# Moving the split weights and one raw buffer by 32 bytes within a partition

## The chip, the cores and the metric

The kernel runs on one core of a Trainium2 chip. The metric is the device time of one execution in microseconds (us); the lower, the better. Two such numbers are compared by the median of their runs. TensorE is the matrix engine (PE in the profile, PEld its weight loads), VectorE (DVE), ScalarE (ACT) and GpSimd (POOL) are the others, and SyncE (SP) issues the DMAs.

## The reference, cut to what matters

Two blocks run one after the other on 256 tokens of width 1024, all in fp32. The first is a convolution mixer and a mixture of 32 experts, the second has two layers of three kinds of attention, a cross attention to a memory, and a gated feed-forward part. The change touches only the second block, where nearly all work is products of the tokens with large weights:

```python
for l in range(DEPTH_2):                       # 2 layers
    xn = rmsnorm_2(x, norm_mix[l])
    (qa, ka, va, ..., gates) = jnp.split(xn @ w_in[l], offsets, axis=-1)      # 1024 x 8004
    ...                                        # attention A, B, C
    y = (g[:, :, 0] * (o_a @ w_up_a[l]) + g[:, :, 1] * (o_b @ w_up_b[l])
         + g[:, :, 2] * (o_c @ w_up_c[l]))
    x = x + y @ w_out[l]
    x = x + memory_cross_attention(rmsnorm_2(x, norm_cross[l]), mem_n, ...)
    x = x + swiglu(rmsnorm_2(x, norm_ffn[l]), w_gu[l], w_down[l])             # 1024 x 5632, 2816 x 1024
return rmsnorm_2(x, final_norm)
```

## The kernel before

Tokens are kept transposed: the 128 partitions hold channels, the free dimension holds the 256 tokens. Each product of the second block is made from parts of the fp32 operands that TensorE takes in its float32r form: a weight chunk is split into a high part (`w_hi`) and the rest (`w_lo`), the tokens into `h_hi` and `h_lo` (both in the tensor `h_parts`) or, in the feed-forward part and for two of the three attention outputs, `act_hi` and `act_lo` (`act_parts`). Three matmuls then stand for one: high x high, low x high, high x low.

The weights come in 35 pieces per layer, each up to 2 MB, by SyncE's queue into three raw buffers in turn: two lie in `raw_a`, the third is `raw_b`. A piece is cut into chunks of 128 x 1024. For each chunk ScalarE copies the raw numbers to `w_hi` (L1616), VectorE, or GpSimd for 26 of the chunks, writes the difference to `w_lo` (`low_part`, L636), and TensorE reads both. `w_hi` and `w_lo` hold four chunks each (`PARTS`). `WORK_SPLIT` is an order written out by hand, the same for all engines, and semaphores (`w_hi_ready`, `w_lo_ready`, `chunk_used`) hold them together.

The lines that read split weights: L990, L991 and L993 (`split_chunk`), L1021 to L1083 (the first products behind a norm), L1416 to L1418 (values, with the tokens as the stationary operand and 512 weight columns moving), L1522 to L1526 (`up`), L1594 to L1597 and L1384 to L1386 (`down`). Two lines read raw buffers as plain fp32: L1546 and L1553 `raw_a`, L1568 `raw_b`.

In the first block the experts' weights stream through `ring` (six slots of 16 KB in a partition) and two spare places, the tensors `wp` and `hs`. L1259 and L1324 multiply them with gathered tokens. The gather (L1222) and the scatter (L1249) are float32r products of which both operands lie in `moe_parts`. `ring` is freed before the tensors of the second block are laid out, so these lie in the same bytes: slot 0 is `w_lo`, slot 1 `w_hi`, slot 2 `raw_b`, slot 3 about `h_parts`, slots 4 and 5 about `raw_a`. Tensors are laid out one behind the other in the order of the `sb(...)` calls. In bytes of a partition they begin at:

| tensor | begins at | rest of a division by 64 |
|---|---|---|
| `ring`, `w_lo` | 1152 | 0 |
| `w_hi` | 17536 | 0 |
| `raw_b` | 33920 | 0 |
| `h_hi` (in `h_parts`, 50304, plus 8 elements) | 50336 | 32 |
| `raw_a` | 66752 | 0 |
| `hs` | 107712 | 0 |
| `act_parts`, `moe_parts` and `big` (one place, at different times) | 145056 | 32 |
| `outs` | 194208 | 32 |
| `wp` | 206496 | 32 |

`H_SHIFT` is 8 elements, 32 bytes. `view(t, at, ...)` gives a part of a tensor from element `at` on, in the shape asked for.

Of the kernel before, what the change touches and what calls it, by code (L numbers as in the profile page):

```python
# [11 lines left out]
F32R = mybir.dt.float32r  # L12
# [6 lines left out]
P = 128  # L19
SEQ = 256  # L20
D = 1024
KD = D // P
# [26 lines left out]
PARTS = 4  # L49
# [4 lines left out]
H_SHIFT = 8  # L54
# [283 lines left out]
def build(nc, x, mem, cst, vec1, vec2, relpad, w_in, w_out, w1, w3, w2, w_in_2, w_up_a, w_up_b, w_up_c,  # L338
# [12 lines left out]
    with ExitStack() as ctx:  # L351
        def sb(name, shape, dt=F32):
            return ctx.enter_context(nc.sbuf_tensor(name, shape, dt))
# [4 lines left out]
        def view(t, at, *dims):  # L358

            n = int(np.prod(dims))  # L360
            ap = t[:, at:at + n]
            if len(dims) == 2:
                return ap.rearrange("p (a b) -> p a b", a=dims[0])
            if len(dims) == 3:
                return ap.rearrange("p (a b c) -> p a b c", a=dims[0], b=dims[1])
            return ap
# [4 lines left out]
        with ExitStack() as first_block:  # L371

            ring = first_block.enter_context(nc.sbuf_tensor("ring", [P, RING, PIECE], F32))
        w_lo = sb("w_lo", [P, PARTS, KD * P], F32R)
        w_hi = sb("w_hi", [P, PARTS, KD * P], F32R)
        raw_b = sb("raw_b", [P, PIECE])
        h_parts = sb("h_parts", [P, 2 * KD * SEQ + 2 * H_SHIFT], F32R)
        h_hi, h_lo = (view(h_parts, H_SHIFT + i * KD * SEQ, KD, SEQ) for i in range(2))
        raw_a = sb("raw_a", [P, RAW - 1, PIECE])
        xT = sb("xT", [P, KD, SEQ])  # L380
        hs = sb("hs", [P, 2 * KD * SEQ])
# [2156 lines left out]
```

How the kernel before makes its waits and increments, by code:

```python
        def enter(eng, name, l=0):  # L556
            d, n = seats[name]
            eng.wait_ge(duo_free[d], l * layer_tenancies[d] + n + 1)
# [1 line left out]
        def freed(eng, name, l=0):  # L561
            d, n = seats[name]
            eng.wait_ge(duo_free[d], l * layer_tenancies[d] + n + 2)
# [7 lines left out]
        def done_piece(eng, i):  # L572
            if i < 2:
                eng.wait_ge(half_done, i + 3)
            else:
                eng.wait_ge(piece_done, i - 1)
# [1 line left out]
        def arrived(eng, i):  # L578
            eng.wait_ge(ring_full[MIX_SLOTS[i]], MIX_SLOTS[:i + 1].count(MIX_SLOTS[i]) * 16)
# [9 lines left out]
        def rotate(eng, r, l):  # L589
            sines, turned_sines = rope_parts(r)
            eng.wait_ge(rope_tmp, l * 5 + r + 1)
            if r >= 2:
                eng.wait_ge(rope_ready, l * 5 + r - 1)
            for at in range(0, P, 32):
                eng.dma_start(turned_sines[at:at + 32], sines[at ^ 32:(at ^ 32) + 32]
                              ).then_inc(rot_odd if r % 2 else rot_even, 16)
# [1 line left out]
        def rotation_in(eng, r, l):  # L600
            if r % 2:
                eng.wait_ge(rot_odd, (l * 2 + r // 2 + 1) * 64)
            else:
                eng.wait_ge(rot_even, (l * 3 + r // 2 + 1) * 64)
# [4 lines left out]
        def raw_arrived(eng, i, l):  # L610
            so_far = sum(LOADS[j] for j in range(i % RAW, i + 1, RAW))
            a_layer = sum(LOADS[j] for j in range(i % RAW, N_LAYER, RAW))
            eng.wait_ge(raw_full[i % RAW], (l * a_layer + so_far) * 16)
```

## Time and profile before

| | us |
|---|---|
| median of 3 runs | 1640.3 |
| lowest and highest | 1639.52, 1641.46 |
| the profiled execution | 1638.12 |
| its span, first to last instruction | 1636.1 |
| TensorE busy | 1562.6 (96%) |
| VectorE busy | 893.3 (55%) |
| ScalarE busy | 651.5 (40%) |

A page of the profile has the busy times, the span in 40 slices, and the chain of work that ended last. Groups of instructions carry their line in the kernel, out<-in by tensor name, the shapes, the count, the time busy and the mean duration of one in ns. A matmul is pipelined: the next one begins before the last has ended, so the mean duration is not the time that one more costs. For that the timeline is read, which gives the start of each instruction; where equal instructions follow each other, one row merges them, with their count and the time from the first start to the last end.

### The profile page before, as it was taken

The numbers are of one execution on the slowest core, as the hardware profiler recorded it, in microseconds if no ns is written. First come the engines' busy times: TensorE is split into PE (matmuls) and PEld (weight loads), VectorE is DVE, ScalarE is ACT, GpSimd is POOL, SyncE is SP. The second block draws the span as 40 slices with busy tenths as digits, with TensorE's granted clock in tenths as the row PEclk, the third lists the DMA queues.
The fourth block names the chain that finished last, engine by engine and source line by source line (L and its number), as shares of the span: only waits on it lengthen the run. The fifth ranks groups of instructions, "written<-read, shape, count | busy, mean of one in ns | idle before, by whom it ended". The sixth has DMA issues, their size and how long they took to land.

```text
span 1636.1 us, 25662 instructions
## 1 busy us (share of the span) xinstructions
PE 1562.6 (96%) x10931; PEld 1255.8 (77%) x10931; DVE 893.3 (55%) x1302; ACT 651.5 (40%) x1022; POOL 62.6 (4%) x30
## 2 busy tenths in 40 slices
PE   8998989889989999999999999999999999999998
PEld 7886434434435349988889799999989889899998
DVE  6933212112111148667887576647566879576654
ACT  2034112112201126454764554435454664464443
POOL 0000000000000000024000000000007000000000
PEclk9988999999999999999999999999999999999999
DMA  9165999999999995626334566474634543265550
GB/s 350 49 252 206 417 428 428 428 428 429 429 429 427 427 402 199 206 104 199 136 117 142 165 196 197 165 259 157 210 122 156 180 155 130 85 215 190 181 205 28
DMA packets 126913, 393.79 MB, mean 241 GB/s; under 512 B 4320, under 2 KB 60000, under 8 KB 114016
## 3 DMA queue, kind: packets, MB, share of 16 engines
q1 hardware_dynamic: 126816, 392.38, 63.5%
q8 instruction: 75, 1.23, 0.3%
q14 instruction: 22, 0.18, 0.0%
HBM read 386.34 MB, written 1.05 MB: 237 GB/s over the span
## 4 chain that ended last, share of the span: by engine, by line
PE 73%; DVE 12%; DMA 10%; ACT 2%; issue 1%; SPq 0%; DVEq 0%; ACTq 0%
PE psum L1259 11%; PE psum L990 10%; PE psum L991 10%; PE psum L993 10%; DMA ring<-w 8%; PE psum L1324 4%; DVE outs L1984 3%; PE psum L1596 2%; PE psum L1594 2%; DVE w_lo L636 2%; PE psum L1597 2%; PE psum L1222 2%; PE psum L1417 1%; PE psum L1418 1%; PE psum L1416 1%; PE psum L951 1%
## 5 line engine op out<-in xcount | busy, mean ns | idle before, releaser
L990 PE MATMUL psum<-h_parts,w_hi 128*128 128x256 f32 x1472 | 358.2, 283 | 0.1
L991 PE MATMUL psum<-h_parts,w_lo 128*128 128x256 f32 x1472 | 352.5, 279 | 0.0
L636 DVE TENSOR_TENSOR w_lo<-raw_a,w_hi 128x1024 fp32r<-128x1024 f32 x184 | 221.9, 1222 | 114.7 <-ACT w_hi L1616 114.0
L990 PEld LDWEIGHTS psum<-h_parts,w_hi 128*128 128x128 f32 x1472 | 276.3, 188 | 6.1 <-issue 5.4
L991 PEld LDWEIGHTS psum<-h_parts,w_lo 128*128 128x128 f32 x1472 | 277.2, 188 | 0.2
L1616 ACT ACTIVATE w_hi<-raw_a 128x1024 fp32r<-128x1024 f32 x202 | 210.4, 1055 | 160.1 <-PE psum L993 62.7
L993 PE MATMUL psum<-h_parts,w_hi 128*128 128x256 f32 x1472 | 201.9, 279 | 0.0
L1259 PE MATMUL psum<-ring,outs 128*64 128x512 f32 x720 | 167.2, 621 | 26.0 <-DMA ring<-w 24.8
L993 PEld LDWEIGHTS psum<-h_parts,w_hi 128*128 128x128 f32 x1472 | 184.7, 188 | 0.0
L1259 PEld LDWEIGHTS psum<-ring,outs 128*64 128x64 f32 x720 | 58.5, 143 | 132.0 <-issue 132.0
L1616 ACT ACTIVATE w_hi<-raw_b 128x1024 fp32r<-128x1024 f32 x100 | 104.8, 1056 | 90.4 <-PE psum L993 52.7
L2185 DVE SCALAR_TENSOR_TENSOR qk<-psum,rtok,qk 128x512 f32<-128x512 f32 x16 | 18.2, 1138 | 220.0 <-PE psum L1259 220.0
L636 DVE TENSOR_TENSOR w_lo<-raw_b,w_hi 128x1024 fp32r<-128x1024 f32 x92 | 111.2, 1222 | 48.8 <-ACT w_hi L1616 48.4
L1324 PE MATMUL psum<-ring,qk 128*64 128x512 f32 x512 | 113.2, 594 | 0.0
L2178 DVE SCALAR_TENSOR_TENSOR moe_parts<-psum,rtok,moe_parts 128x512 fp32r<-128x512 f32 x34 | 24.1, 747 | 141.4 <-ACT moe_parts L1613 141.4
L636 POOL TENSOR_TENSOR w_lo<-raw_a,w_hi 128x1024 fp32r<-128x1024 f32 x18 | 43.3, 2429 | 1316.6 <-ACT w_hi L1616 1316.6
L1616 ACT ACTIVATE qk<-psum 128x512 f32<-128x512 f32 (+2 forms) x28 | 16.7, 597 | 189.6 <-PE psum L1302 163.9
L1596 PE MATMUL psum<-act_parts,w_hi 128*128 128x256 f32 x328 | 91.6, 279 | 0.0
L1594 PE MATMUL psum<-act_parts,w_hi 128*128 128x256 f32 x328 | 91.6, 279 | 0.0
L1597 PE MATMUL psum<-act_parts,w_lo 128*128 128x256 f32 x328 | 91.6, 279 | 0.0
L1324 PEld LDWEIGHTS psum<-ring,qk 128*64 128x64 f32 x512 | 36.9, 137 | 62.7 <-issue 62.6
L911 PE MATMUL psum<-hs,ring 128*128 128x256 f32 x320 | 69.4, 379 | 0.0
(310 smaller groups left out, 2535.0 us busy)
## 6 DMA issues: line engine op xcount, KB each, us to landing
ring<-w SPq DMA_DIRECT2D x76, 2048.0 KB, 16.4
raw_a<-w_in SPq DMA_DIRECT2D x20, 2048.0 KB, 7.9
raw_a<-w_gu SPq DMA_DIRECT2D x32, 1024.0 KB, 7.8
raw_b<-w_in SPq DMA_DIRECT2D x10, 2048.0 KB, 8.9
wp<-w SPq DMA_DIRECT2D x8, 2048.0 KB, 18.7
hs<-w SPq DMA_DIRECT2D x8, 2048.0 KB, 23.1
raw_b<-w_gu SPq DMA_DIRECT2D x12, 1024.0 KB, 7.6
raw_a<-w_down SPq DMA_DIRECT2D x8, 1536.0 KB, 6.6
```

The source lines that it names most:

```text
L636: return eng.tensor_tensor(chunk_part(w_lo, n), chunk_raw(n), chunk_part(w_hi, n).bitcast(F32), ALU.subtract)
L911: last = mm(view(duo(name), 0, 4, SEQ)[:, o, :], w[:, k, o * P:(o + 1) * P], hT[:, k, :], start=(k == 0 and o % 2 == 0), stop=(k == KD - 1 ...
L990: mm(to, hi[:, k, :], h_hi[:, k, :], start=(k == 0), stop=False)
L991: mm(to, lo[:, k, :], h_hi[:, k, :], start=False, stop=False)
L993: last = mm(to, hi[:, k, :], h_lo[:, k, :], start=False, stop=(k == KD - 1))
L1259: last = mm(psum[rows, d, bank * 512:bank * 512 + 512], duo_tokens[k // 4][:, k % 4, cols], view(places[e], 0, KD, D_EXPERT)[:, k, :], sta ...
L1324: last = mm(psum[rows, 2, half * 512:half * 512 + 512], hidT[:, f, rows], view(ring[:, at + e, :], 0, 4, D)[:, f, half * 512:half * 512 + ...
L1594: mm(to, hi[:, o, :], act_hi[:, k, :], start=(k == 0 and o % 2 == 0), stop=False, skip_group_check=True)
L1596: mm(to, hi[:, o, :], act_lo[:, k, :], start=False, stop=False, skip_group_check=True)
L1597: last = mm(to, lo[:, o, :], act_hi[:, k, :], start=False, stop=(k == KF - 1), skip_group_check=True)
L1616: return nca.activation(out_ap, in_ap, ACT.Copy)
L1984: ins = v.scalar_tensor_tensor(dst[:, k, :], src[:, k, j:j + SEQ], tap, dst[:, k, :], ALU.mult, ALU.add)
```

## The change

The two tensors `w_lo` and `w_hi` become one, `w_parts`, with 8 elements of room ahead, in which `w_lo` comes first and `w_hi` behind it. The 8 elements that `h_parts` had ahead of `h_hi` are taken away. So `w_lo`, `w_hi` and `raw_b` begin 32 bytes later, at 1184, 17568 and 33952, and `h_hi` and all behind it stay where they are. No instruction is added, removed or moved.

```diff
-        w_lo = sb("w_lo", [P, PARTS, KD * P], F32R)
-        w_hi = sb("w_hi", [P, PARTS, KD * P], F32R)
+        w_parts = sb("w_parts", [P, H_SHIFT + 2 * PARTS * KD * P], F32R)
+        w_lo, w_hi = (view(w_parts, H_SHIFT + i * PARTS * KD * P, PARTS, KD * P) for i in range(2))
         raw_b = sb("raw_b", [P, PIECE])
-        h_parts = sb("h_parts", [P, 2 * KD * SEQ + 2 * H_SHIFT], F32R)
-        h_hi, h_lo = (view(h_parts, H_SHIFT + i * KD * SEQ, KD, SEQ) for i in range(2))
+        h_parts = sb("h_parts", [P, 2 * KD * SEQ + H_SHIFT], F32R)
+        h_hi, h_lo = (view(h_parts, i * KD * SEQ, KD, SEQ) for i in range(2))
         raw_a = sb("raw_a", [P, RAW - 1, PIECE])
```

## Rows read from the trace of the kernel before

**Rows 1.** The page: busy us and share of the span, DMA share in 40 slices.

```profile
PE 1562.6 (96%) x10931; PEld 1255.8 (77%) x10931; DVE 893.3 (55%) x1302; ACT 651.5 (40%) x1022; POOL 62.6 (4%) x30
...
DMA  9165999999999995626334566474634543265550
```

**Rows 2.** The page: the chain that ended last, shares of the span by line.

```profile
PE psum L1259 11%; PE psum L990 10%; PE psum L991 10%; PE psum L993 10%; DMA ring<-w 8%; PE psum L1324 4%; DVE outs L1984 3%; PE psum L1596 2%; PE psum L1594 2%; DVE w_lo L636 2%; PE psum L1597 2%; PE psum L1222 2%; PE psum L1417 1%; PE psum L1418 1%; PE psum L1416 1%; PE psum L951 1%
```

**Rows 3.** TensorE's waits, 610 to 1636 us: total us, times, longest.

```profile
PE psum L1477 <- DVE wp L2372: 9.7, 10, 1.9
PE psum L1477 <- DVE wp L2368: 3.7, 6, 1.0
```

**Rows 4.** Groups by line and form on TensorE: count, busy us, mean ns, idle before.

```profile
L990 PE MATMUL psum<-h_parts,w_hi 128*128 128x256 f32 x1472 | 358.2, 283 | 0.1
...
L1594 PE MATMUL psum<-act_parts,w_hi 128*128 128x256 f32 x328 | 91.6, 279 | 0.0
...
L1417 PE MATMUL psum<-w_lo,h_parts 128*128 128x512 f32 x96 | 38.0, 395 | 0.0
...
L1522 PE MATMUL psum<-act_parts,w_hi 128*128 128x256 f32 x128 | 31.5, 281 | 0.8 <-ACT outs L1616 0.8
```

**Rows 5.** A stretch of the feed-forward part: busy us of each engine, clock, DMA.

```profile
950.00:1110.00 160.00, 160.00 (x1374) 160.00 (x1373) 98.41 (x101) 73.50 (x81) 0.00 (x0) 1.00 0.58 194
```

**Rows 6.** Timeline of TensorE, 730 to 734 us: start, us, what, count.

```profile
730.00 0.28 PE L991 MATMUL psum<-h_parts,w_lo 128*128 128x256 f32 x1
...
731.28 1.10 PE L993 MATMUL psum<-h_parts,w_hi 128*128 128x256 f32 x8
...
733.97 0.28 PE L991 MATMUL psum<-h_parts,w_lo 128*128 128x256 f32 x1
```

**Rows 7.** Timeline of TensorE in the second layer's attention, 1222 to 1230 us.

```profile
1224.73 0.39 PE L990 MATMUL psum<-h_parts,w_hi 128*128 128x256 f32 x1
1224.95 0.28 PE L991 MATMUL psum<-h_parts,w_lo 128*128 128x256 f32 x1
...
1226.60 0.28 PE L991 MATMUL psum<-h_parts,w_lo 128*128 128x256 f32 x1
```

**Rows 8.** Timeline of TensorE in the first layer's values, 635 to 641 us.

```profile
635.51 0.39 PE L1416 MATMUL psum<-w_hi,h_parts 128*128 128x512 f32 x1
...
640.87 0.40 PE L1418 MATMUL psum<-w_hi,h_parts 128*128 128x512 f32 x1
```

**Rows 9.** Timeline of TensorE in the experts, 491 to 496 us.

```profile
491.54 0.52 PE L1249 MATMUL psum<-moe_parts 128*128 128x256 f32 x3
491.90 4.00 PE L1222 MATMUL psum<-moe_parts 128*128 128x256 f32 x32
```

**Rows 10.** Timeline of TensorE in the experts, a whole half of a scatter.

```profile
254.03 1.21 PE L1249 MATMUL psum<-moe_parts 128*128 128x256 f32 x8
```

**Rows 11.** Timeline of TensorE, plain fp32 matmuls of 256 columns, from 900 us.

```profile
899.68 1.46 PE L1546 MATMUL psum<-memT,raw_a 128*128 128x256 f32 x6
```

**Rows 12.** Groups by form on TensorE: the experts' matmuls from the spare places.

```profile
L1259 PE MATMUL psum<-wp,outs 128*64 128x512 f32 x120 | 52.9, 592 | 0.0
L1259 PE MATMUL psum<-hs,outs 128*64 128x512 f32 x120 | 52.9, 592 | 0.0
```

**Rows 13.** Groups by form on VectorE and ScalarE, the same shape in different tensors.

```profile
L636 DVE TENSOR_TENSOR w_lo<-raw_b,w_hi 128x1024 fp32r<-128x1024 f32 x92 | 111.2, 1222 | 48.8 <-ACT w_hi L1616 48.4
...
L2403 DVE TENSOR_TENSOR act_parts<-outs,act_parts 128x1024 fp32r<-128x1024 f32 x4 | 4.9, 1221 | 0.1
...
L1616 ACT ACTIVATE w_hi<-raw_b 128x1024 fp32r<-128x1024 f32 x100 | 104.8, 1056 | 90.4 <-PE psum L993 52.7 <-PE psum L1597 24.3 <-PE psum L1083 6.9
...
L1616 ACT ACTIVATE act_parts<-outs 128x1024 fp32r<-128x1024 f32 x4 | 4.2, 1056 | 1.4 <-DVE outs L2398 1.4
```

**Rows 14.** DMA issues: what, count, KB each, median us from issue to landing.

```profile
wp<-w SPq DMA_DIRECT2D x8, 2048.0 KB, 18.7
hs<-w SPq DMA_DIRECT2D x8, 2048.0 KB, 23.1
```

## Prediction

> **What bounds the kernel now.** I read the page first: TensorE is busy for 96% of the span, VectorE for 55%, ScalarE for 40%, and the DMA engines are full only up to about 600 us [rows 1]. The chain that ended last then names the lines: it is mostly TensorE, and the two largest lines that read the split weights, L990 and L991, have 10% each, as has L993 [rows 2]. So two regimes stand side by side. Up to about 614 us the experts stream their weights from HBM into `ring`; the change doesn't touch an address there. Behind that come the two layers, some 1020 us, in which TensorE multiplies split weights. Here the engine hardly waits: from 610 us to the end the largest wait in total is 9.7 us, in ten pieces, for VectorE's probabilities, the next 3.7 us, in six [rows 3]. What counts is therefore how long one matmul of split weights takes from its start to the start of the next.
>
> The "mean ns of one" of the groups doesn't tell this: it is 279 ns for a 256-column matmul [rows 4], since matmuls overlap. I take starts instead. In the stretch 950 to 1110 us, gate and up products (L990 to L993) and behind them the down products (L1594 to L1597), TensorE is without a gap and begins 1374 matmuls [rows 5]; less the two or so that reach in from before, that is 160.00 / 1371.6 = 116.7 ns each. Single stamps say the same: from 730.00 to 733.97 us lie 34 starts (11, then the 8 of L993, then 15), 3.97 / 34 = 116.8 ns [rows 6]. In the attention stage a second pace is seen, 1224.95 to 1226.60 us with 14 starts, 117.9 ns; it holds for one chunk of weights and the next may be back at 116.7 [rows 7]. The 512-column forms (L1416 to L1418) take 635.51 to 640.87 us for 23 starts, 233.0 ns, twice the 116.5 [rows 8]. At 2.4 GHz, the level that is granted there (PEclk 1.00 [rows 5]), 256 columns would be 106.7 ns if one went in per cycle. Some 10 ns in each matmul are thus a stall, and that stall is what an address could change.
>
> **What the change does to addresses.** `ring` and `w_lo` begin at byte 1152 of a partition, a multiple of 64. Before: `w_lo` 1152, `w_hi` 17536, `raw_b` 33920, all multiples of 64 ("even" below); `h_hi` and `h_lo` 32 bytes past one ("odd"). After: `w_lo` 1184, `w_hi` 17568, `raw_b` 33952, all odd; `h_hi` stays at 50336 and all behind it stays as well. `act_parts` and `moe_parts` begin at 145056, odd in both kernels. No instruction, wait or byte of traffic is added or removed, and the order on every queue is the same. What changes is this: each split matmul had one operand even and one odd; now both are odd.
>
> **Part by part.** *Matmuls.* The trace of before has a fp32r matmul with both operands odd: the experts' gather (L1222) and scatter (L1249), stationary and moving both from `moe_parts`, 128x128 by 256 columns, at the full clock. L1222 takes (4.00 - 0.28) / 31 = 120.0 ns per start, and the last three starts of L1249 ahead of it 0.36 us, 120 ns as well [rows 9]. L1249 comes in short rows of 8: 1.21 us, of which 0.28 are the last one and some 0.22 the first start behind another form (as 1224.73 to 1224.95 us [rows 7]), leaves 0.71 / 6 = 118.3 ns [rows 10]. So the nearest rows give +3.3 ns where the pattern has locked, +1.6 ns where it hasn't. Is it the DMA traffic of the experts' stage that slows L1222? The pace of 116.7 ns holds over 160 us in which the DMA share is 0.58 [rows 5], which speaks against a load-dependent stall, though not at a share of 0.9. Is it the moving operand alone? That one is odd in L990 and in L1222 alike, and even in L1417, and L990 and L1417 have the same pace per column [rows 6, 8]. What differs is the relation of the two. I take 120.0, since the rows of 8 to 24 and more of the layers resemble the 32 of L1222 more than the 8 of L1249.
>
> The count: L990, L991 and L993 1472 each, 4416; L1594, L1596 and L1597 328 each, 984; and 19 smaller forms of the same view with 24 to 128 each, of which L1522 is the largest, together 1272 [rows 4]. That is 6672 of 256 columns. 6672 x 3.3 = 22.0 us. The 288 of 512 columns: 240.0 - 233.0 = 7.0 ns each, 2.0 us. Sum 24.0 us, all on TensorE.
>
> What of it is not seen at the end: some starts already have the slower pace (117.9), and, by an estimate from the 24 matmuls between two changes of form in attention [rows 7], about one start in forty is such a change with its own 0.2 us, in which a stall of 3 ns vanishes; I take 1.5 us off. In attention TensorE waits 16 times for VectorE (L1477), up to 1.9 us each [rows 3]; with 24 matmuls of gates between two units it comes 24 x 3.3 = 0.08 us later itself, so these waits give back 0.08 us each, 1.3 us. Net 21.2 us, a share of 1.3% of the profiled run. If that cover is gone, because VectorE is late by the same amount, it is 22.5 us.
>
> One rule of the Trainium skill speaks against this sum. The page "SBUF — State Buffer", section "Operand start alignment", says that a start at a multiple of the element size is legal and that this is "about legality, not speed", and its section on bandwidth pools says that contention is structural, between port pairs, while TensorE has a port of its own for the moving and one for the stationary operand. By that, an address would cost nothing and the sum would be 0. The page "TensorE: Matmul & The Clock Gate", section "Back-to-back issue gap", gives about 109 ns for 256 columns; the trace disagrees here (116.7 ns). [...]
>
> *Other readers and writers of the moved tensors.* Plain fp32 matmuls don't mind: L1259 has its moving operand odd (`wp`) or even (`hs`) beside an odd `outs`, and both take 592 ns [rows 12]. That prices the 64 of L1568, which read `raw_b`, at 0. ScalarE: `w_hi<-raw_b` (even from even) 1056 ns, `act_parts<-outs` (odd from odd) 1056 ns, the same shape; VectorE: `w_lo` 1222 ns, L2403 in `act_parts` 1221 ns [rows 13]. So 0 for the 302 splits and 276 differences; even 10 ns each would be 3 us on engines that aren't the bound, of which a few tenths show. GpSimd's 26 low parts have no row at an odd place; I bound them by the two ends that VectorE shows, nothing either way. *DMA.* `wp` (odd) and `hs` (even) are filled as a pair, 2 MB each, and land 18.7 and 23.1 us from issue, the second behind the first by 4.4 us as its bytes need [rows 14]; no sign that an odd place costs. With a DMA share near 0.5 in the layers, `raw_b` could take a microsecond more per load before anyone waited. In the region shared with `ring` the last 32 bytes of each tensor now lie in the next slot, whose reader is done by then: 0.
>
> **The rivals.** *Half a stall.* The patterns don't lock at 120 but at L1249's pace: 6672 x 1.6 = 10.7 us, with the 512-column forms 11.7, less 1.5: +10, 1651 us. For it: the layers show more than one pace already, and their starts come from forms like those before L1249. Against it: once L1249 or L1222 runs on, it is at 120 (491.54 to 491.90 us, three starts [rows 9]).
>
> *No effect.* The 120 ns belong to `moe_parts` for another reason, for instance because both operands lie in the same 28 KB of a partition, while weights and tokens lie in different stretches of it in before as in after. Then the time is 1640 us, within 0.2%. It is also what the rule of the Trainium skill's page "SBUF — State Buffer" amounts to. For it: no row has two odd operands in two different tensors. Against it: `w_hi` with `h_parts` and `w_hi` with `act_parts` are some 33 and 128 KB apart and share the one pace of that stretch [rows 5], so distance did nothing there, and parity is the plainest difference left.
>
> *Faster.* The stall of 10 ns is a crossing that arises because the operands lie in different halves of 64 bytes, and it vanishes when they agree. Its place is every split matmul, its price at most 116.7 - 106.7 = 10 ns, 67 us in all, down to about 1573 us, since VectorE and ScalarE, busy for 98 and 74 of 160 us there [rows 5], don't bind. It decides if L1222's 120 ns has a cause of its own that outweighs the gain. The rows of L1222 speak directly against it.
>
> *The change doesn't do what it says*: the tensors are rounded up so that `raw_b` or `h_parts` land elsewhere. The sizes are multiples of 32 bytes, so I give this nothing of its own; it would look like no effect.
>
> **How the numbers follow.** The profiled run took 1638.1 us, its span 1636.1, and 2.0 lie around it; the median of three is 1640.3, 2.2 above. 1638.1 + 21.2 = 1659.3, on the median 1661.5; I say 1661. Chances: locked pace 0.54 (1655 to 1665), half a stall 0.21 (1645 to 1655), no effect 0.19 (1638.5 to 1642), faster 0.04, something slower still 0.02. Leaving out at most 2 in 10 takes the lower end to 1640 and the upper one to 1665, which also holds the sum without cover. Slower by over 0.2% (1643.6; about what a measurement of this kernel can tell from no change) 0.77, within it 0.19, faster 0.04.
>
> **What would show it.** Right: in the profile of after L1222 is still 120.0 ns, the starts of L990 to L993 stand 120 ns apart in the gate and up products, 160 us there hold about 1333 starts, L1416 to L1418 240 ns apart, and the span up to 614 us is the same. Half a stall: 118.3 ns, and the pattern changes from chunk to chunk. Wrong: 116.7 ns as before, or the extra time stands in waits of TensorE for `w_hi`, `w_lo` or a DMA into `raw_b`. If the pace is 120 and the end moved by less than 15 us, my account of the cover failed.

## The result and the profile after

| | before | after |
|---|---|---|
| median, 4 runs each, same chip | 1639.91 us | 1653.51 us |
| lowest and highest | 1638.95, 1641.46 | 1652.75, 1654.74 |
| the profiled execution | 1638.12 | 1654.74 |
| its span | 1636.1 | 1652.7 |

The ratio of the medians' runs is 1.0085, 95% interval 1.0073 to 1.0097: slower by 13.6 us by the medians, and by 16.6 us by the two profiled executions. I ran the changed kernel once more, on another occasion, to see how firm that is.

> The changed kernel itself, beside the kernel before on the chip of the next two. All theories: 1653 to 1656 us; the sum by starts of the first profile says +16 us for the layers, the first four runs said +13.6. If the profiled execution's experts' stage (up to 614 us) again agrees with before within 1 us and the layers are 16 us longer, the missing 3 us are spread between runs and no term of the sum.

Measured: 1655.18 us (1652.46 to 1655.9, 4 runs) beside 1639.83 us for the kernel before (9 runs), ratio 1.0095, interval 1.0078 to 1.0112, span 1652.5 us. So the change costs 14 to 15 us by the medians and 16.4 to 16.6 by the profiled spans, and the mean paces below came out the same to 0.01 ns in both profiled executions.

First the page of after, its engines and the chain by line. TensorE is at 96% as in [rows 1], VectorE did the same 893.3 us of work, and the chain has the same lines as [rows 2].

```profile
PE 1584.6 (96%) x10931; PEld 1278.5 (77%) x10931; DVE 893.3 (54%) x1302; ACT 651.0 (39%) x1022; POOL 62.1 (4%) x30
```

TensorE's waits from 610 us on, the two lines that answer to [rows 3], and a third one in after and then in before. They have all become shorter, so the loss isn't a wait.

```profile
PE psum L1477 <- DVE wp L2372: 9.0, 8, 1.9
PE psum L1477 <- DVE wp L2368: 3.4, 6, 1.0
PE psum L1083 <- ACT h_parts L1613: 1.4, 2, 0.7
```

```profile
PE psum L1083 <- ACT h_parts L1613: 2.5, 2, 1.2
```

The groups that answer to [rows 4]: count, busy us, mean ns of one. The 256-column forms went from 283 to 286 ns and from 279 to 283 ns; the 512-column form went the other way, from 395 to 390 ns.

```profile
L990 PE MATMUL psum<-h_parts,w_parts 128*128 128x256 f32 x1472 | 366.0, 286 | 0.0
...
L1594 PE MATMUL psum<-act_parts,w_parts 128*128 128x256 f32 x328 | 92.8, 283 | 0.0
...
L1417 PE MATMUL psum<-w_parts,h_parts 128*128 128x512 f32 x96 | 37.4, 390 | 0.0
```

The same 160 us of the feed-forward part as in [rows 5], which lie some 10 us later now: 1336 starts instead of 1374, 160.00 / 1334 = 119.9 ns each.

```profile
960.00:1120.00 160.00, 160.00 (x1336) 160.00 (x1335) 94.59 (x97) 69.71 (x76) 0.00 (x0) 1.00 0.56 187
```

And single starts, in the timeline of TensorE (start us, us, what, count), as in [rows 6], [rows 8] and [rows 9].

```profile
731.83 0.28 PE L990 MATMUL psum<-h_parts,w_parts 128*128 128x256 f32 x1
...
732.79 1.12 PE L993 MATMUL psum<-h_parts,w_parts 128*128 128x256 f32 x8
...
735.55 0.28 PE L991 MATMUL psum<-h_parts,w_parts 128*128 128x256 f32 x1
```

```profile
636.51 0.40 PE L1416 MATMUL psum<-w_parts,h_parts 128*128 128x512 f32 x1
...
641.75 0.39 PE L1418 MATMUL psum<-w_parts,h_parts 128*128 128x512 f32 x1
```

```profile
492.58 4.00 PE L1222 MATMUL psum<-moe_parts 128*128 128x256 f32 x32
```

From 731.83 to 735.55 us lie 31 starts, 3.72 / 31 = 120.0 ns. From 636.51 to 641.75 us lie 23, 227.8 ns. L1222, which nothing of the change touches, is at 120.0 ns as before.

I took the gap between every start and the next from both traces. Among the split matmuls of 256 columns there are 6503 gaps of at most 130 ns in before and 6505 in after (the rest are changes of form, waits and missing records). Their mean is 116.81 ns in before and 119.86 in after. In after, each run of them settles after one to nine gaps at 120, 120, 120; in before there are three patterns, 117, 117, 116 and one that begins 113, 116, 118, 120 (both with a mean of 116.7), and 118, 119, 116, 119, 119, 116 (mean 117.8). Of 77 runs of a dozen gaps or more in before, 56 end at 116.7 and 21 at 117.8. The account of the profiled spans:

| | us |
|---|---|
| steady gaps, 6505 x 3.055 ns | +19.9 |
| 512-column forms, 282 gaps, 233.18 to 227.26 ns | -1.7 |
| starts behind another form or a wait | -1.8 |
| the rest (L1568 +0.7, others -0.5) | +0.2 |
| sum | +16.6 |

It comes where the split matmuls run: the same instruction starts 0.7 us later at 605 us and 0.2 us earlier at 614, 2.5 later at 880, 4.5 at 945, 9.4 at 1120 (the feed-forward part of the first layer alone is 5 us), 11.6 at 1431 and 16.6 at the end.

### The profile page after: what moved, and what is told of

Its sections match the earlier page's. It is cut to its first block, busy times and chain, and to the rows that moved or that the text cites. A ratio compares the mean times of both kernels' runs of the same rounds, so it can differ in the third digit from the quotient of the medians.

```text
span 1652.7 us, 25662 instructions
## 1 busy us (share of the span) xinstructions
PE 1584.6 (96%) x10931; PEld 1278.5 (77%) x10931; DVE 893.3 (54%) x1302; ACT 651.0 (39%) x1022; POOL 62.1 (4%) x30
## 4 chain that ended last, share of the span: by engine, by line
PE 76%; DVE 11%; DMA 10%; ACT 2%; issue 1%; SPq 0%; DVEq 0%; ACTq 0%
PE psum L1259 11%; PE psum L990 10%; PE psum L993 10%; PE psum L991 10%; DMA ring<-w 8%; PE psum L1324 4%; DVE outs L1984 3%; PE psum L1597 2%; PE psum L1596 2%; PE psum L1594 2%; DVE w_parts L636 2%; PE psum L1222 2%; PE psum L1416 1%; PE psum L1417 1%; PE psum L1418 1%; PE psum L1021 1%
## 5 line engine op out<-in xcount | busy, mean ns | idle before, releaser
L990 PE MATMUL psum<-h_parts,w_parts 128*128 128x256 f32 x1472 | 366.0, 286 | 0.0
L991 PE MATMUL psum<-h_parts,w_parts 128*128 128x256 f32 x1472 | 360.5, 283 | 0.0
L636 DVE TENSOR_TENSOR w_parts<-raw_a,w_parts 128x1024 fp32r<-128x1024 f32 x184 | 221.9, 1222 | 123.0 <-ACT w_parts L1616 122.3
L990 PEld LDWEIGHTS psum<-h_parts,w_parts 128*128 128x128 f32 x1472 | 281.8, 191 | 5.8 <-issue 5.1
L991 PEld LDWEIGHTS psum<-h_parts,w_parts 128*128 128x128 f32 x1472 | 281.9, 191 | 0.2
L1616 ACT ACTIVATE w_parts<-raw_a 128x1024 fp32r<-128x1024 f32 x202 | 210.2, 1053 | 168.1 <-PE psum L993 67.6
L993 PE MATMUL psum<-h_parts,w_parts 128*128 128x256 f32 x1472 | 206.4, 283 | 0.0
L993 PEld LDWEIGHTS psum<-h_parts,w_parts 128*128 128x128 f32 x1472 | 189.9, 192 | 0.0
L1616 ACT ACTIVATE w_parts<-raw_b 128x1024 fp32r<-128x1024 f32 x100 | 104.5, 1053 | 95.7 <-PE psum L993 56.0
L636 DVE TENSOR_TENSOR w_parts<-raw_b,w_parts 128x1024 fp32r<-128x1024 f32 x92 | 111.3, 1222 | 52.0 <-ACT w_parts L1616 51.5
L1594 PE MATMUL psum<-act_parts,w_parts 128*128 128x256 f32 x328 | 92.8, 283 | 0.0
L1596 PE MATMUL psum<-act_parts,w_parts 128*128 128x256 f32 x328 | 92.8, 283 | 0.0
L1597 PE MATMUL psum<-act_parts,w_parts 128*128 128x256 f32 x328 | 92.8, 283 | 0.0
L636 POOL TENSOR_TENSOR w_parts<-raw_a,w_parts 128x1024 fp32r<-128x1024 f32 x18 | 42.7, 2402 | 1326.6 <-ACT w_parts L1616 1326.6
```

Source lines behind the costliest of these rows:

```text
L636: return eng.tensor_tensor(chunk_part(w_lo, n), chunk_raw(n), chunk_part(w_hi, n).bitcast(F32), ALU.subtract)
L990: mm(to, hi[:, k, :], h_hi[:, k, :], start=(k == 0), stop=False)
L991: mm(to, lo[:, k, :], h_hi[:, k, :], start=False, stop=False)
L993: last = mm(to, hi[:, k, :], h_lo[:, k, :], start=False, stop=(k == KD - 1))
L1594: mm(to, hi[:, o, :], act_hi[:, k, :], start=(k == 0 and o % 2 == 0), stop=False, skip_group_check=True)
L1596: mm(to, hi[:, o, :], act_lo[:, k, :], start=False, stop=False, skip_group_check=True)
```

## The experiments

Throughout, "distance" is where the stationary operand begins, less where the moving one begins, as a rest of a division by 256 bytes. For the 256-column forms `w_hi` and `w_lo` are stationary and tokens move. In before it is 224 for `h_parts` (1152 less 50336) and 224 for `act_parts` (1152 less 145056); in after 0 for both. For the 512-column forms, where the weights move, it is 32 in before and 0 in after. All slices are multiples of 512 bytes long, so that it holds for each of them. This way to see it came last; the first experiments asked for less.

**Same place or odd place?** The tokens go back to a multiple of 64, where the weights are in before: both even. If being odd were the cause, the time would be that of before.

```diff
-        h_hi, h_lo = (view(h_parts, H_SHIFT + i * KD * SEQ, KD, SEQ) for i in range(2))
+        h_hi, h_lo = (view(h_parts, i * KD * SEQ, KD, SEQ) for i in range(2))
```

> The split weights, raw_b and h_parts all begin at a multiple of 64 bytes; act_parts stays 32 bytes past one. Theory A (the relation counts: the stall differs when stationary and moving operand agree in the rest by 64 bytes): L990, L991 and L993 start 120.0 ns apart as in the changed kernel, L1594 to L1597 116.7 ns as in the kernel before, L1416 to L1418 227 ns; of 6672 matmuls of 256 columns about 5230 are 3.1 ns slower, 16 us, less 1.7 us for the 512-column ones and what the engine waits less: about 1651 us, a little under the changed kernel. Theory B (an odd stationary operand is what costs): 116.7 ns everywhere, 1640 us. Theory C (both must be odd): 116.7 ns everywhere, 1640 us.

Measured: 1653.32 us (1649.08 to 1656.08, 4 runs), ratio 1.0071, interval 1.0052 to 1.009. The forms that read `h_parts` take 119.90 ns, the 512-column ones 227.25, the ones that read `act_parts`, whose relation is that of before, 117.8 (L1594 to L1597) and 117.3 (L1522 to L1526), where I had expected 116.7: the slower of the two paces seen in before. So neither parity as such nor the new bytes of the weights make the 120 ns; that both operands are at the same place does. Its groups, the same columns as above:

```profile
L990 PE MATMUL psum<-h_parts,w_hi 128*128 128x256 f32 x1472 | 366.3, 287 | 0.0
...
L1594 PE MATMUL psum<-act_parts,w_hi 128*128 128x256 f32 x328 | 91.8, 280 | 0.0
...
L1416 PE MATMUL psum<-w_hi,h_parts 128*128 128x512 f32 x96 | 37.4, 390 | 0.0
```

**Weights odd, tokens elsewhere.** The weights stay where the change puts them, the tokens move on by 32 bytes as well (50368); `act_parts` stays.

```diff
-        h_hi, h_lo = (view(h_parts, i * KD * SEQ, KD, SEQ) for i in range(2))
+        h_hi, h_lo = (view(h_parts, H_SHIFT + i * KD * SEQ, KD, SEQ) for i in range(2))
```

The diff is against the changed kernel.

> The split weights and raw_b stay 32 bytes past a multiple of 64 as in the changed kernel, h_parts goes back to a multiple of 64. Theory A (relation): L990 to L993 116.7 ns, L1416 to L1418 233 ns, only L1594 to L1597 and the matmuls with act_parts (984 + 384 + 72 of 256 columns) at 120.0 ns: 1440 x 3.1 = 4.5 us over the kernel before, 1644 us. Theory B (an odd stationary operand costs): L990 to L993 stay at 120.0 ns, about 1654 us.

Measured: 1642.07 us (1639.57 to 1646.46, 10 runs), ratio 1.0012, interval 1.0002 to 1.0022, some 2.7 us over before where 4.5 were expected. `h_parts` is back at 116.82 ns and the 512-column forms at 233.26, while `act_parts`, still at the weights' place, takes 119.96. Its timeline in the down products: 35 starts in 4.20 us, 120.0 ns.

```profile
1074.76 0.28 PE L1596 MATMUL psum<-act_parts,w_parts 128*128 128x256 f32 x1
...
1078.96 0.28 PE L1594 MATMUL psum<-act_parts,w_parts 128*128 128x256 f32 x1
```

The two experiments are each other's mirror: each brings one group to 120 ns and leaves the other one below it.

**The raw buffer alone.** Only `raw_b` begins 32 bytes later.

```diff
-        raw_b = sb("raw_b", [P, PIECE])
-        h_parts = sb("h_parts", [P, 2 * KD * SEQ + 2 * H_SHIFT], F32R)
-        h_hi, h_lo = (view(h_parts, H_SHIFT + i * KD * SEQ, KD, SEQ) for i in range(2))
+        raw_b = sb("raw_b", [P, H_SHIFT + PIECE])[:, H_SHIFT:]
+        h_parts = sb("h_parts", [P, 2 * KD * SEQ + H_SHIFT], F32R)
+        h_hi, h_lo = (view(h_parts, i * KD * SEQ, KD, SEQ) for i in range(2))
```

> Only raw_b begins 32 bytes later; the split weights stay at multiples of 64. Theory A: 116.7 ns everywhere and the time of the kernel before, 1640 us, with the splits of raw_b (L1616) at 1056 ns and L1568 unchanged. Rival D (part of the 13.6 us is paid by the reader or the DMA of raw_b): up to some us over the kernel before, and L1616, L636 from raw_b, L1568 or the landing times of raw_b differ.

Measured: 1639.32 us (10 runs), ratio 0.9998, interval 0.9988 to 1.0007; the mean pace is 116.8 ns as in before, and L1568, which reads `raw_b` in plain fp32, starts every 215.9 ns at the full clock in both. The third part of the change costs nothing that can be measured. But the runs of starts didn't settle alike: 9 of the 77 have a mean over 0.3 ns off before, most of them by about 1 ns and in both directions (34 gaps behind 870 us 117.9 ns instead of 116.8, 22 gaps behind 901 us 116.9 instead of 117.8), though no operand of theirs lies elsewhere.

**The pace by itself.** A kernel of its own: rows of 64 float32r matmuls, 128x128 stationary, each row with its own offsets (in elements of 4 bytes) into a moving and a stationary tensor.

```python
for j in range(64): pe.matmul(*at(256, 0, 0, j), **last(j))    # columns, moving, stationary: same place
for j in range(64): pe.matmul(*at(256, 0, 8, j), **last(j))    # stationary 32 bytes on
```

> A kernel of its own, not the computation: it leaves the whole reference out and only runs rows of 64 float32r matmuls, 128x128 stationary, one row for each pair of places of the two operands, each on its own line, with two small plain matmuls between rows. Theory A: of 256 columns, rows whose operands agree in the rest by 64 bytes take 120.0 ns per start, rows 32 bytes apart 116.7 to 118 ns, for even and odd moving operand alike, and 64 bytes apart is as 0. Of 512 columns 227 ns where they agree and 233 ns where they are 32 bytes apart; of 128 columns, if the stall is 32 cycles of 2.4 GHz per weight load, 66.7 ns where they agree. Offsets of 4 to 28 bytes: open; a stall that follows 32-byte lines would put them between or at the one or the other. Rival C (the absolute place counts): the rows with the moving operand at 0 differ from those at 32 bytes for the same distance.

Its timeline: start us, us for the 64, line. L61 has both operands at the same place, L77 the stationary one 32 bytes on, L93 64 bytes on, L97 the moving one 32 bytes on, L101 both 32 bytes on, L109 the moving one 64 bytes on, L117 both 16 bytes on. Then 512 columns (L125 same place, L129 32 bytes apart), 128 columns (L141) and 384 (L151).

```profile
31.05 7.92 PE L61 MATMUL psum<-moving,stationary 128*128 128x256 f32 x64
...
95.25 7.82 PE L77 MATMUL psum<-moving,stationary 128*128 128x256 f32 x64
...
159.24 7.52 PE L93 MATMUL psum<-moving,stationary 128*128 128x256 f32 x64
...
175.00 7.71 PE L97 MATMUL psum<-moving,stationary 128*128 128x256 f32 x64
...
190.87 7.92 PE L101 MATMUL psum<-moving,stationary 128*128 128x256 f32 x64
...
223.01 7.50 PE L109 MATMUL psum<-moving,stationary 128*128 128x256 f32 x64
...
254.78 7.82 PE L117 MATMUL psum<-moving,stationary 128*128 128x256 f32 x64
...
286.86 14.80 PE L125 MATMUL psum<-moving,stationary 128*128 128x512 f32 x64
...
317.23 15.19 PE L129 MATMUL psum<-moving,stationary 128*128 128x512 f32 x64
...
409.13 7.34 PE L141 MATMUL psum<-moving,stationary 128*128 128x128 f32 x64
...
447.10 11.35 PE L151 MATMUL psum<-moving,stationary 128*128 128x384 f32 x64
```

Over the last 32 starts of a row that is 120.0 ns at the same place (also 32 or 64 bytes on in both), 118.3, 113.3 and 116.7 ns for L77, L93 and L97, and 113.3 for L109; 226.7 against 233.3 ns with 512 columns. With 384 columns it is 173.3 ns and with 128 columns 111.7, at each of the places tried; for the same place I had put 66.7 ns down for 128 columns, a miss. While the rows run, no other engine is busy and the DMA share is 0.00, so the stall is TensorE's own. Rival C isn't quite gone: with both operands 16 bytes on (L117) the same place costs 118.3 ns and not 120.0, in a pattern of its own, so that at 16 bytes the absolute place has a say as well. And there is more than one good place: 64 bytes apart, either way round, took 113.3 ns, less than the steady pace of the split matmuls in the kernel before.

**Using it: tokens 64 bytes off the weights.** I took that 113.3 ns to the kernel: the tokens at 50368, which makes the distance 192.

```diff
-        h_hi, h_lo = (view(h_parts, H_SHIFT + i * KD * SEQ, KD, SEQ) for i in range(2))
+        h_hi, h_lo = (view(h_parts, 2 * H_SHIFT + i * KD * SEQ, KD, SEQ) for i in range(2))
```

> Weights and raw_b as in the kernel before; h_hi and h_lo begin 64 bytes past a multiple of 128 instead of 32, so they are 64 bytes from the weights; act_parts stays. The offset rows gave 113.3 ns for 64 bytes (both at multiples of 64), 120.0 for 0 and 116.7 or 118.3 for 32. Theory A2 (the relation counts within 128 bytes, and the offset rows carry over): L990 to L993 and all with h_parts stand 113.3 ns apart, 5232 matmuls x 3.4 = 18 us less than before: 1622 us; L1594 to L1597 unchanged at 116.7. Theory A (only the rest by 64 counts): 120.0 ns, 1655 us as with all at multiples of 64. If the kernel's own order of matmuls (two stationary parts for one moving) breaks the pattern: 116.7 and no gain.

Measured: 1650.24 us (1646.63 to 1652.04, 4 runs), ratio 1.0071, interval 1.0054 to 1.0088; 117.58 ns for `h_parts`, 118.22 for the down products. A miss, and in the wrong direction. And `act_parts`, which didn't move, has two paces of its own: in the down products of the first layer 116.7 ns as in before, in those of the second 120.0, 35 starts in 4.20 us:

```profile
1589.74 0.28 PE L1594 MATMUL psum<-act_parts,w_hi 128*128 128x256 f32 x1
...
1593.94 0.28 PE L1597 MATMUL psum<-act_parts,w_lo 128*128 128x256 f32 x1
```

So 120 ns isn't the mark of the same place alone: a distance of 224 can settle there too. Only part of the 10.4 us is in the paces: 6502 x 0.85 ns = 5.5 us; L1568, at another clock in some of its starts (below), has 1.5 us, and 1.5 us are there at 614 us already. The profiled execution itself took 8.4 us more in its span.

With one buffer of 32 bytes laid out ahead of `act_parts`, these are 64 bytes off as well (distance 192 for all):

```diff
         v2 = sb("v2", [P, N_VEC2])
+        top8 = sb("top8", [P, 8])
...
-        top8 = sb("top8", [P, 8])
```

> As the last, and act_parts (with all behind it) 32 bytes later, at 64 bytes past a multiple of 128, by laying out the 32-byte tensor top8 ahead of it. Theory A2: L1594 to L1597 and L1522 to L1526 too at 113.3 ns, 6672 x 3.4 = 23 us less than before, 1617 us. Theory A: 120.0 ns everywhere, 1661 us.

Measured: 1645.84 us (6 runs), ratio 1.0037, interval 1.0024 to 1.0049, a second miss. The large groups are at 117.5 to 117.8 ns. But of 76 runs of a dozen gaps or more, 8 end at 113.3 ns, as hoped, and nearly all others at 117.8. The same operands have more than one stable pattern.

**The period.** A second kernel of rows, with larger and other offsets.

> A kernel of its own, not the computation: it leaves the whole reference out and runs rows of 64 float32r matmuls as the first one, for more places. Theory A2 (period of 128 bytes): of 256 columns 113.3 ns for 64, 192, 320 and 448 bytes of distance, 120.0 for 128, 256 and 384; the same for moving ahead of stationary. If the period is longer, 128 bytes differs from 0. Last three rows: the kernel's own order, two stationary parts for one moving operand, at 0, 32 and 64 bytes: 120.0, 118.3, 113.3.

L67 has the stationary operand 64 bytes on, the pair that had taken 113.3 ns (7.52 us) in the first such kernel, and now takes 117.8; L73 has it 256 bytes on. L129 and L131 are 512 columns with 192 and 256 bytes.

```profile
39.02 7.78 PE L67 MATMUL psum<-moving,stationary 128*128 128x256 f32 x64
...
63.04 7.92 PE L73 MATMUL psum<-moving,stationary 128*128 128x256 f32 x64
...
294.93 14.92 PE L129 MATMUL psum<-moving,stationary 128*128 128x512 f32 x64
310.04 14.81 PE L131 MATMUL psum<-moving,stationary 128*128 128x512 f32 x64
```

All pairs 256 bytes apart, in either direction, took 120.0 ns, and 226.7 with 512 columns. 64 bytes apart took 113.3 or 117.8, 192 bytes apart 117.8, and 128 bytes apart 118.5 or 118.7, but 120.0 in two of six rows. So the rest by 256 is what brings the pace of the same place back each time, not that by 64, by 32 or, as I had expected, by 128. The kernel's own order gave 120.0, 118.3 and 117.8 ns at 0, 32 and 64 bytes; for the last I had expected 113.3.

**Every distance, in the kernel's own order.** Each of five different lead-ins (a few plain matmuls that shift the moment at which the row begins) is followed by twice the 24 matmuls of a chunk, in the order of L990, L991 and L993, for distances 0, 4, ... 252 bytes.

> A kernel of its own, not the computation: it leaves the whole reference out. For each distance of 0 to 252 bytes between stationary and moving operand, in steps of 4, it runs the kernel's own order of 24 matmuls of 256 columns (high and low part for one moving operand, then the high parts) twice, behind five different lead-ins of plain matmuls. The offset rows gave two paces for the same distance of 64 bytes, 113.3 and 117.8 ns. Theory E (each distance has a few stable patterns, and the phase at entry picks one): the five rows of one distance differ at 64 bytes and at 32, while distance 0 gives 120.0 ns whatever the lead-in, and 256 bytes is the period, so no distance from 4 to 252 bytes is 120.0 in all five save by chance. If one distance gives 113.3 behind every lead-in, a kernel laid out by it would be 6672 x 3.4 = 23 us faster than before. Against E: every distance has one pace, and the 117.8 came from another cause.

The means of the last 24 gaps, each behind the five lead-ins:

```
distance   0  120.0 120.0 120.0 120.0 120.0
           4  118.4 118.4 118.3 118.3 118.3
           8  115.5 115.5 115.6 115.5 115.5
          52  113.3 120.0 113.3 113.4 113.3
          64  117.8 117.8 113.3 113.3 117.8
          76  113.3 113.4 113.3 113.3 113.3
         100  120.0 120.0 120.0 120.0 120.0
         192  117.7 117.8 117.8 117.8 117.8
         224  117.8 116.6 117.8 117.8 116.7
         252  120.0 120.0 120.0 120.0 120.0
```

Three of these rows are known from the kernels. 0 is after, 119.9. 224 is before, and it has the two paces that I read in [rows 6] and [rows 7]. 192 is the kernel with the tokens 64 bytes off, 117.6: in the kernel's own order it settles at 117.8 behind all five lead-ins. Equal matmuls in a row at this distance had taken 113.3 in the first kernel of rows (L109) and 117.8 in the second, so my bet was on one of its two patterns, and the kernel is mostly in the other; which one a run takes I can't foretell. Half of what I had expected failed: at 32 bytes all five rows are alike (118.3 to 118.4), and ten distances other than 0 have 119.9 or 120.0 behind every lead-in (20, 36, 84, 100, 156, 160, 216, 228, 244 and 252), far more than chance. The same place is thus one costly place among several. Distances of 76 and of 52 bytes look best; only the first has 113.3 behind all five lead-ins. In the timeline (start, us for 48), 0 is L70 and 76 is L108:

```profile
56.62 6.00 PE L70 MATMUL psum<-moving,stationary 128*128 128x256 f32 x48
...
700.21 5.69 PE L108 MATMUL psum<-moving,stationary 128*128 128x256 f32 x48
```

**Distance 76 in the kernel.** The weights begin at 1164, the tokens at 50496, `act_parts` at 145216. Three small late buffers (not four, as I wrote ahead of the run) were moved into the gaps; besides the places nothing changes.

```diff
-        w_lo = sb("w_lo", [P, PARTS, KD * P], F32R)
-        w_hi = sb("w_hi", [P, PARTS, KD * P], F32R)
+        w_parts = sb("w_parts", [P, 3 + 2 * PARTS * KD * P], F32R)
+        w_lo, w_hi = (view(w_parts, 3 + i * PARTS * KD * P, PARTS, KD * P) for i in range(2))
         raw_b = sb("raw_b", [P, PIECE])
-        h_parts = sb("h_parts", [P, 2 * KD * SEQ + 2 * H_SHIFT], F32R)
+        stat = sb("stat", [P, 3, 6])
+        top8 = sb("top8", [P, 8])
+        h_parts = sb("h_parts", [P, 2 * KD * SEQ + H_SHIFT], F32R)
...
         v2 = sb("v2", [P, N_VEC2])
+        lam = sb("lam", [P, 8])
...
-        stat = sb("stat", [P, 3, 6])
...
-        top8 = sb("top8", [P, 8])
-        lam = sb("lam", [P, 8])
```

> The kernel before with the stationary weight parts 76 bytes behind the moving operands by their places mod 256 bytes, for all three groups (weight parts at 1164, high and low tokens at 50496, activation parts at 145216; four small buffers moved to make room, nothing else changed). Theory, distance mod 256 bytes decides: the rows of 24 matmuls at 76 bytes took 113.3 ns each, all five of them, so 6672 split matmuls take 113.3 instead of 116.8 ns, 23 us less, some of which later waits take back: 1617 to 1625 us, L990 to L997 at about 275 ns by the profile's groups and starts 113.3 ns apart. Rival 1, only being at the same place mod 64 or 32 bytes counts and all else is 116.7 to 117.8 ns: 1640 to 1645 us. Rival 2, the pace of a row in a kernel of its own doesn't carry over, as in e4_h_64_apart where 113.3 was expected and 117.6 came: 1636 to 1650 us, with 116.7 to 118.3 ns. Matmuls of 512 columns stay at 233.3 ns in both.

Measured: 1626.91 us (1625.55 to 1628.08, 5 runs) beside 1639.84 (9 runs), ratio 0.9924, interval 0.991 to 0.9937: 13 us faster than the kernel before, and 27 us faster than the changed one. The steady gaps have a mean of 113.66 ns (6473 of them). Its feed-forward stretch has 1415 starts in the 160 us of [rows 5]; the two rows of L993 are 24 starts apart, 2.73 / 24 = 113.8 ns.

```profile
950.00:1110.00 160.00, 160.00 (x1415) 160.00 (x1414) 100.42 (x103) 75.40 (x82) 0.00 (x0) 1.00 0.61 205
```

```profile
1001.63 1.07 PE L993 MATMUL psum<-h_parts,w_parts 128*128 128x256 f32 x8
...
1004.36 1.07 PE L993 MATMUL psum<-h_parts,w_parts 128*128 128x256 f32 x8
```

The end lies above the 1617 to 1625 us that I had put down. In the gaps, 6473 x 3.15 ns = 20.4 us are gained, but the span is only 12.2 us shorter. 6 of 79 runs of a dozen gaps or more sit at 120.0 ns after all (they are in the mean). All split starts together, those behind a change of form or a wait included, gain 15.6 us. Of the 4.8 us between, 1.6 are 16 gaps of 213 ns in a stretch at the lower clock (from 1199 us, below), about 1.5 are waits that before doesn't have (0.8 us for VectorE's `w_parts`, at L990 and L1522, and 0.7 at L1083), and the rest is lost elsewhere at changes of form. L1568 gives back another 3.6 us: it reads `raw_b` in plain fp32, and 21 of its starts are some 427 ns apart (416 to 559) instead of 216, against 4 in before. That is a matter of the clock. The timeline of L1568, before and then this kernel:

```profile
1431.14 8.19 PE L1568 MATMUL psum<-outs,raw_b 128*128 128x256 f32 x32 [0.42 <-issue]
```

```profile
1422.79 9.62 PE L1568 MATMUL psum<-outs,raw_b 128*128 128x256 f32 x32 [0.43 <-issue]
```

And the windows of this kernel: ahead of L1568 TensorE is busy for 2.44 of 4.80 us, then the granted clock is 0.50, the lower of its two levels, for its first 3.40 us. It is 0.50 as well from 1199.20 to 1202.40 us, in the middle of a chunk of L990 and L991; in before it is 1.00 in that stretch.

```profile
1418.00:1422.80 4.80, 2.44 (x23) 1.61 (x21) 0.86 (x2) 2.70 (x9) 0.00 (x0) 0.81 1.09 356
1422.80:1426.20 3.40, 3.40 (x8) 2.77 (x9) 1.99 (x2) 2.95 (x3) 0.00 (x0) 0.50 1.10 348
```

```profile
1199.20:1202.40 3.20, 3.20 (x17) 3.20 (x17) 0.68 (x3) 1.95 (x7) 0.00 (x0) 0.50 0.70 263
```

L1568 takes 15.9 us in before, 16.6 and 15.4 in the two profiled executions of the changed kernel and 19.0 in the both-even one; where the clock falls differs from execution to execution, and I have no experiment that binds it to an address. Four of the five runs of this kernel have a mean granted clock of 0.976 and the fifth 0.981, those of before beside it 0.980 to 0.984, so it isn't the profiled execution alone. The account of the span: -15.6 + 3.6 (L1568) - 0.7 (512 columns, distance 180) + 0.5 (all other lines) = -12.2 us.

## Why the prediction was right, and where it wasn't

**Direction and mechanism held.** The stages, the count, the idea that the relation of two operands sets the pace, and L1222 as the row to go by: in after all split matmuls are at L1222's 120.0 ns. The stretch of 160 us held 1336 starts where I had said about 1333, L1222 stayed, and at 614 us the two are within 1 us of each other. Waits for `w_hi`, `w_lo` or a DMA into `raw_b` didn't appear. Raw buffer, splits and DMA were put at 0, and the raw buffer alone gave 0.9998. For the plain fp32 matmuls I had read mean durations, which I had myself called a poor sign; the starts of L1568, 215.9 ns apart with `raw_b` at either place, are the better one.

**The size: 21.2 us said, 16.6 in the profiled spans, 13.6 and 15.4 by the medians.** The terms of the sum, one by one:

- 6672 x 3.3 = 22.0 us. The difference was 3.05 ns, since before has some runs at 117.8, and since after needs up to nine starts until it sits at 120. 6672 x 3.05 = 20.3 us, 1.7 less.
- 288 x 7.0 ns = +2.0 us for 512 columns. This is the step that failed, in its sign. It measured -1.7 us. I had scaled the stall with the columns. The rows say otherwise: at the same place the extra is 120.0 - 106.7 = 13.3 ns with 256 columns, 173.3 - 160.0 = 13.3 with 384, and 227.3 - 213.3 = 14 with 512. For these three lengths it is about 13 ns for each matmul, some 32 cycles of 2.4 GHz, and not so much per column; that isn't a law either, for with 128 columns it is 111.7 - 53.3 = 58.4 ns. In before it was 10 ns with 256 columns and 20 with 512, at distances of 224 and 32. "233.0 is twice 116.5" was a coincidence that looked like a law.
- What isn't seen at the end: -2.8 us said (1.5 for starts at a change of form or slower already, 1.3 for waits). All split starts together cost 18.1 us, so 2.2 of the 20.3 didn't show (1.8 of the 19.9 in the table, which counts the steady gaps alone), about half of it in the wait of L1083 for ScalarE (2.5 to 1.4 us), which I had not counted. The waits at L1477 went from 9.7 and 3.7 us to 9.0 and 3.4; they stand in the 0.2 us of the rest.

That makes 20.3 - 1.7 - 2.2 + 0.2 = 16.6 us. My own test said that under 15 us at a pace of 120 the account of the cover has failed. The first pair of medians, 13.6 us, falls under it, the second, 15.4, and the spans, 16.6 and 16.4, don't. By the traces the cover took about what it was said to take, in part at another wait. The term that failed is the 3.7 us between +2.0 and -1.7. The first medians differ by 3 us less than the profiled executions because the profiled one of before was 1.8 us under its median and that of after 1.2 us over it, both within the spread between runs (all runs of before lie between 1636.86 and 1642.38); after's had the lowest granted clock of its four runs (0.980 against 0.983 to 0.985). That some of the good aim is luck should be said: 1653.5 us lies in the band that I gave to *half a stall* (1645 to 1655), and only the second median, 1655.2, just in that of the locked pace.

**The rivals.** *Half a stall*: the time fits it, but the pattern did lock, at 120.0 ns in nearly all longer runs. *No effect*: fell with the both-even kernel, which has no operand of that group in `moe_parts` and none at an odd place, and takes 119.9 ns. The Trainium skill's page "SBUF — State Buffer", section "Operand start alignment", calls its alignment rule one about legality, not speed, and adds that its runs timed nothing; so it leaves the speed open, and my "an address would cost nothing" went beyond it. What the runs here speak against is that conclusion, also as drawn from the two read ports of TensorE in its section on bandwidth pools: three kernels with the same instructions differ by 27 us through the starts alone. *Faster*: wrong for this change, yet its core, that the stall belongs to the pair and that another pair can lose it, is what the last kernel used: 113.7 instead of 116.8 ns. Its floor of 106.7 ns wasn't seen at any distance; the Trainium skill's page "TensorE: Matmul & The Clock Gate", section "Back-to-back issue gap", has 262 cycles, about 109 ns, for 256 columns as the gap of an isolated matmul, and the lowest stable pace of these float32r matmuls with a weight load each is 113.3.

**The rule that I argued with was too small.** "Even and odd" by 64 bytes happened to give the right forecast, because after has distance 0 in every group, and so has L1222: its operands lie in one tensor, all at multiples of 256 bytes from its start. What the runs support in its place is the distance by 256 bytes, for moving operands that begin at a multiple of 32 bytes, and even that gives a set of patterns and not one pace. A rule of the same kind, by 128 bytes, lay behind the bet of 1622 us on a kernel that came to 1650.

## What to carry to other kernels

Where TensorE is saturated with float32r matmuls that each load their weights, read the gap between starts, not the mean duration, and compare it with columns / 2.4: what is over may hang on where the two operands begin, as a distance by 256 bytes. With 256 columns the same place is among the costly ones; measure the distances in the kernel's own order and behind several lead-ins, since one distance can have several stable patterns, and a row of equal matmuls may show the wrong one. Don't scale such a stall to another length, neither by the column nor by the matmul: measure a row of each length.

## What the runs showed of the hardware that I had not expected

- The pace of a 256-column float32r matmul with its weight load takes any of several values, such as 113.3, 115.5, 116.7, 117.8, 118.3, 120.0 and up to 123.4 ns, and 4 bytes of distance already change it: 0, 4 and 8 bytes give 120.0, 118.3 and 115.5.
- One distance can hold several patterns: 64 and 192 bytes have 113.3 and 117.8 ns each, and 224 has 116.7, 117.8 and, with operands that hadn't moved, 120.0.
- With 512 columns the same place is the best of those tried (226.7 against 228.8 to 233.3 ns), with 256 it is among the costly ones; with 128 columns every place tried took 111.7 ns, with 384 173.3.
- At distance 0 the mean repeats to 0.01 ns between two executions of the changed kernel. Where a distance has several patterns it needn't: before and the kernel with `raw_b` alone moved have the same mean (116.81 and 116.82 ns), but 9 of 77 runs of starts settled otherwise. Whether two executions of one such kernel agree line by line, no pair of traces here shows.

Why TensorE stalls by the two starts stays open. That the load of the next stationary operand and the stream of the moving one meet in the same part of memory is a guess. Moving both operands by 32 or 64 bytes left the pace at 120.0 ns, which would fit it; moving both by 16 bytes gave 118.3, which it doesn't explain, and no run shows what happens inside.
